# A two-block layer on one core: routing from the unnormalised residual, the first expert's places from its ranks, and two weight loads moved into the mixer

## What is computed

```python
h = h + hybrid_mixer(rmsnorm(h, norm_mix), ...)
hn = rmsnorm(h, norm_ffn)                      # x * rsqrt(mean(x*x) + eps) * g
g_logits = hn @ w_router_group                 # 256 x 4
g_idx = argmax(g_logits); g_w = softmax(g_logits)[g_idx]
e_sel = (hn @ w_router_expert)[group g_idx]    # 8 logits
top_v, top_i = top_k(e_sel, 2)
gates = g_w * softmax(top_v)
# for each token and each of its two experts e:
out += gate * ((silu(hn @ w_gate[e]) * (hn @ w_up[e])) @ w_down[e])
h = h + out
```

## Time and profile before

| what | value |
|---|---|
| median of 3 runs | 996.39 us (995.67 to 996.49) |
| the profiled execution: its time | 996.21 us |
| the profiled execution: its span | 994.5 us |
| mean granted TensorE clock | 0.918 |
| PE busy, PE weight load busy | 795.2 us (80%), 604.5 us (61%) |
| DVE, ACT, POOL busy | 476.2, 315.8, 90.2 us |
| moved by DMA | 287.00 MB, mean 289 GB/s |
| chain that ended last | DMA 36%, PE 33%, issue 21%, DVE 4% |

### The profile page before, as it was taken

One profiled execution on the slowest core, in us unless ns is written; L12 is line 12 of the kernel. 1 busy time (PEld: TensorE's weight loads), 2 busy tenths in 40 slices (PEclk: granted clock), 3 DMA queues, 4 the chain that ended last, 5 costly groups with the idle time before them and its releaser, 6 DMA issues.

```text
span 994.5 us, 15637 instructions
## 1 busy us (share of the span) xinstructions
PE 795.2 (80%) x6490; PEld 604.5 (61%) x6490; DVE 476.2 (48%) x823; ACT 315.8 (32%) x513; POOL 90.2 (9%) x111
## 2 busy tenths in 40 slices
PE   6999999998946475646636566577998999999996
PEld 6989998775624243333413334244887888888884
DVE  5856849555322031312203122125747687766775
ACT  6754355631100000000000000004485454444443
POOL 1039554100000000000000000000001010000000
PEclk9999999999988687878879798689999999999998
DMA  9984334458999999999999999999852556555101
GB/s 306 315 289 165 129 127 170 150 203 342 383 426 426 430 427 424 430 426 426 426 426 428 427 426 426 428 426 389 283 168 87 176 184 189 209 196 169 43 2 42
DMA packets 70773, 287.00 MB, mean 289 GB/s; under 512 B 11521, under 2 KB 36398, under 8 KB 58414
## 3 DMA queue, kind: packets, MB, share of 16 engines
q1 hardware_dynamic: 70386, 285.38, 72.9%
q10 hardware_dynamic: 316, 0.58, 0.2%
HBM read 284.90 MB, written 1.05 MB: 288 GB/s over the span
## 4 chain that ended last, share of the span: by engine, by line
DMA 36%; PE 33%; issue 21%; DVE 4%; POOL 3%; ACT 3%; SPq 0%; POOLq 0%; DVEq 0%; ACTq 0%
DMA down_a<-in_w_down_dram 29%; PE bank L575 12%; PE bank L624 5%; PE bank L2072 5%; DMA pair_d<-in_w_up_dram 4%; PE bank L603 3%; PE bank L2055 2%; DMA ring<-in_w_down_dram 2%; PE bank L2045 1%; DVE act_p L522 1%; DVE w_lo L560 1%; PE bank L1902 1%; ACT w_hi L550 1%; POOL seg_r L860 1%; PE bank L612 1%
## 5 line engine op out<-in xcount | busy, mean ns | idle before, releaser
L560 DVE TENSOR_TENSOR w_lo<-ring,w_hi 128x1024 fp32r<-128x1024 f32 x137 | 176.8, 1291 | 118.7 <-ACT w_hi L550 118.5
L550 ACT ACTIVATE w_hi<-ring 128x1024 fp32r<-128x1024 f32 x138 | 146.1, 1059 | 186.6 <-PE bank L575 65.0
L575 PE MATMUL bank<-act_p,w_hi 128*128 128x256 f32 x736 | 141.1, 293 | 8.0 <-issue 7.7
L1610 DVE COPY y_e<-bank 32x256 f32<-32x256 f32 x64 | 27.2, 424 | 239.0 <-PE bank L2072 238.6
L575 PEld LDWEIGHTS bank<-act_p,w_hi 128*128 128x128 f32 x736 | 118.4, 197 | 10.7 <-issue 9.9
L591 PE MATMUL bank<-act_p,w_hi 128*128 128x512 f32 x352 | 122.0, 397 | 0.0
L1118 ACT ACTIVATE y_e<-bank 32x256 f32<-32x256 f32 x64 | 23.9, 374 | 283.3 <-PE bank L2072 282.9
L575 PE MATMUL bank<-act_p,w_lo 128*128 128x256 f32 x368 | 106.1, 288 | 0.0
L2072 PE MATMUL bank<-down_a,h_t 128*32 128x256 f32 x512 | 44.8, 509 | 71.0 <-DMA down_a<-in_w_down_dram 59.7
L2055 PE MATMUL bank<-ring,x_t 128*32 128x256 f32 x1536 | 94.2, 400 | 8.8 <-issue 8.0
L624 PE MATMUL bank<-w_hi,act_q 128*128 128x512 f32 x304 | 95.3, 394 | 0.4 <-issue 0.4
(11 more groups left out here) (356 smaller groups left out, 1032.4 us busy)
## 6 DMA issues: line engine op xcount, KB each, us to landing
ring<-in_w_up_dram SPq DMA_DIRECT2D x24, 2048.0 KB, 35.5
ring<-in_w_gate_dram SPq DMA_DIRECT2D x24, 2048.0 KB, 31.0
down_a<-in_w_down_dram SPq DMA_DIRECT2D x16, 2048.0 KB, 26.1
ring<-in_w_in_dram SPq DMA_DIRECT2D x15, 2048.0 KB, 18.8
down_b<-in_w_down_dram SPq DMA_DIRECT2D x15, 2048.0 KB, 26.1
ring<-in_w_ffn_in_dram SPq DMA_DIRECT2D x22, 1024.0 KB, 6.8
pair_d<-in_w_gate_dram SPq DMA_DIRECT2D x8, 2048.0 KB, 30.1
pair_d<-in_w_up_dram SPq DMA_DIRECT2D x8, 2048.0 KB, 34.9
```

Source lines behind the costliest of these rows:

```text
L550: nc.scalar.activation(parts(w_hi, g, view), view, ACT.Copy).then_inc(split_hi, 1)
L560: engine.tensor_tensor(parts(w_lo, g, view), view, h, ALU.subtract).then_inc(split_lo, 1)
L575: mm = nc.tensor.matmul(dst, parts(wt, g, grans[g][1])[:, k, :], a[:, x_part, k, :], start=(k == 0 and i == 0), stop=(k == KC - 1 and i == 2))
L1610: ins = nc.vector.tensor_copy(y_e[CAP * e:CAP * (e + 1), 256 * j:256 * (j + 1)], bank[2][CAP * j:CAP * (j + 1), 0:256])
```

## The change

Four parts, all between the last quarter of the first mixer and the second expert:

1. **Loads.** `down_a` no longer shares its place with the routing tiles, which become views of `y_e` and `gmat`. Its first load stands behind the third of the six halves; the gate half of `pair_d` stands ahead of the sixth and waits for grain 56, the up half and `down_b` stay behind the mixer.
2. **Routing from `res`.** PE transposes the residual itself (read with a step of 8 elements) as soon as it is added. POOL multiplies `w_rt` with the gain beforehand. The norm's factor is positive and the same for all logits of a token, so the choice does not need it; it goes into the exponentials as their scale. ACT writes both blocks of `tok` beside the routing.
3. **Fewer linked steps.** The best and second of all four groups are found at once, beside the choice of the group; the ranks are divided by 32 with comparisons; gates and number of rounds are worked out later, and the engines load the number after the second group.
4. **First expert.** Expert 0's places are its ranks. A one-hot of 32 columns (`onehot[:, 1]`) is built from them, PE gathers those 32 rows first (`gather_first`), starts the product per half, and gathers the other 96 afterwards. 6 `keep_running` steps stand where there were 14.

```diff
+    down_a = sb("down_a", [P, UNIT], where=ph)
+    rt = y_e[:, 0:12 * TB * NE].rearrange("p (n b e) -> p n b e", n=12, b=TB)
+    r8 = y_e[:, 12 * TB * NE:14 * TB * NE + 32].rearrange("p (n b e) -> p n b e", n=10, b=TB)
+    r1 = y_e[:, 15 * TB * NE:15 * TB * NE + 16 * TB].rearrange("p (n b) -> p n b", n=16)
+    m_lt = gmat[:, 0:P]
...
+    TOK_BANK = ((4, 5), (7, 0))
+    LOGIT_BANK = (6, 1)
...
             load_half(i, n, i)
+            if (i, n) == (0, 1):
+                sp.wait_ge(sc_sum, KC)
+                sp.wait_ge(silu_done, XC)
+                sp.wait_ge(v_used, KC)
+                load_down(0, 0)
+            if (i, n) == (2, 1):
+                sp.wait_ge(gran_used, G_WO + 12)
+                load_half(3, 0, 3)
         sp.wait_ge(gran_used, GA)
-        load_half(3, 0, 3)
         load_half(3, 1, 3)
         load_down(1, 1)
-        sp.wait_ge(routed, 1)
-        load_down(0, 0)
...
+        nc.gpsimd.tensor_tensor(w_rt[:, :, :], w_rt[:, :, :], bcast(g_ffn[:, :].unsqueeze(2), [P, KC, NG + NE]), ALU.mult)
...
         act.wait_ge(res_mix, 1)
-        norm_act(act, 1, res, tok, (res_mix, 2), turned_rows=True)
-        for c in range(0, KC, 2):
-            act.wait_ge(tok_turned, c + 1)
-            nc.scalar.activation(tok_t[:, c, :], bank[c % 4][:, 0:T], ACT.Copy,
-                                 scale=g_ffn[:, c:c + 1]).then_inc(tok_act, 1)
-        act.wait_ge(neg_abs, 3)
-        nc.scalar.activation(r8[:, 5, :, 0:NG], r8[:, 4, :, 0:NG], ACT.Exp).then_inc(exp_ready, 1)
+        nc.scalar.activation(tok[:, 0, :], res[:, 0, :], ACT.Square, accum_out=sm[:, 0:1])
+        act.wait_ge(tok_turned, 1)
+        nc.scalar.activation(*turned_out(0, 0), ACT.Copy).then_inc(tok_act, 1)
+        act.wait_ge(tok_turned, 4)
+        nc.scalar.activation(*turned_out(1, 1), ACT.Copy).then_inc(tok_act, 1)
+        act.wait_ge(res_mix, 2)
+        nc.scalar.activation(tok[:, 1, :], res[:, 1, :], ACT.Square, accum_out=sm[:, 1:2]).then_inc(ss_act, 1)
+        act.wait_ge(rstd_ready, 2)
+        act.wait_ge(ss_act, 2)
+        for b in range(TB):
+            ins = nc.scalar.activation(by_chunk(tok[:, b, :], True), by_feature(res[:, b, :], True), ACT.Copy,
+                                       scale=sm[:, 4 + b:5 + b])
+        ins.then_inc(nrm_act, 1)
         act.wait_ge(neg_abs, 4)
-        nc.scalar.activation(r1[:, 5, :], r1[:, 4, :], ACT.Exp).then_inc(exp_ready, 1)
-        act.wait_ge(routed, 1)
-        n_more = act.value_load(rounds_i[0:1, 2:3], min_val=NE // 8 - 1, max_val=NE // 8 * (T // CAP) - 1)
+        for b in range(TB):
+            nc.scalar.activation(r8[:, 5, b, 0:NG], r8[:, 4, b, 0:NG], ACT.Exp, scale=sm[:, 4 + b:5 + b])
+            ins = nc.scalar.activation(r1[:, 5, b:b + 1], r1[:, 4, b:b + 1], ACT.Exp, scale=sm[:, 4 + b:5 + b])
+        ins.then_inc(exp_ready, 1)
...
-        dve.wait_ge(res_mix, 2)
-        norm_dve(dve, 1, res, tok, turned_rows=True)
-        for c in range(1, KC, 2):
-            dve.wait_ge(tok_turned, c + 1)
-            nc.vector.tensor_scalar(tok_t[:, c, :], bank[c % 4][:, 0:T], g_ffn[:, c:c + 1], None,
-                                    ALU.mult).then_inc(tok_dve, 1)
+        for b, h in ((0, 1), (1, 0)):
+            dve.wait_ge(tok_turned, 2 * b + h + 1)
+            nc.vector.tensor_copy(tok_t[:, 4 * h:4 * h + 4, b * P:(b + 1) * P],
+                                  bank[TOK_BANK[b][h]][:, :].rearrange("p (c t) -> p c t", c=4)).then_inc(tok_dve, 1)
...
         for b in range(TB):
-            ins = nc.vector.tensor_copy(lgt[:, b, :], bank[6 + b][:, 0:NG + NE])
+            dve.wait_ge(logits_raw, b + 1)
+            nc.vector.tensor_copy(by_group(G_LOGIT)[:, b, :], bank[LOGIT_BANK[b]][:, 0:NG])
+            ins = nc.vector.tensor_copy(rt[:, 10, b, :], bank[LOGIT_BANK[b]][:, NG:NG + NE])
+            if b == 0:
+                dve.wait_ge(ss_act, 2)
...
+        nc.vector.tensor_reduce(g_top, by_group(G_LOGIT), AX_X, ALU.max)
+        link_dve(dve, nc.vector.tensor_reduce(groups(TOP_1), experts(10), AX_X, ALU.max))
+        nc.vector.tensor_tensor(by_group(G_EQ), by_group(G_LOGIT), by_token(g_top, NG), ALU.is_equal)
+        link_dve(dve, nc.vector.tensor_tensor(experts(0), experts(10), of_group(groups(TOP_1)), ALU.is_equal))
+        nc.vector.scalar_tensor_tensor(out=by_group(G_AT), in0=by_group(G_EQ), scalar=-100.0, in1=iota_g,
+                                       op0=ALU.mult, op1=ALU.add)
+        link_dve(dve, nc.vector.scalar_tensor_tensor(out=experts(1), in0=experts(0), scalar=-100.0, in1=iota_e,
+                                                     op0=ALU.mult, op1=ALU.add))
+        nc.vector.tensor_reduce(g_at, by_group(G_AT), AX_X, ALU.min)
+        link_dve(dve, nc.vector.tensor_reduce(groups(AT_1), experts(1), AX_X, ALU.min))
+        nc.vector.tensor_tensor(by_group(G_HOT), by_group(G_AT), by_token(g_at, NG), ALU.is_equal)
+        link_dve(dve, nc.vector.tensor_tensor(experts(5), experts(1), of_group(groups(AT_1)), ALU.is_equal))
...
+        first_rank = r8[:, 9, :, 0]
+        link_dve(dve, nc.vector.tensor_copy(first_rank, bank[5][:, 0:TB * NE].rearrange("p (b e) -> p b e", b=TB)[:, :, 0]))
+        for b in range(TB):
+            ins = nc.vector.tensor_scalar(onehot[:, 1, b, 0:CAP], iota_f[:, 0:CAP], r8[:, 9, b, 0:1], rt[:, 4, b, 0:1],
+                                          ALU.is_equal, ALU.mult)
+        ins.then_inc(member, 1)
...
+        def rounds():
+            dve.wait_ge(rank_raw, 2)
+            most, over, more = r1[:, 8, 0:1], r8[:, 0, 0, 0:7], r1[:, 9, 0:1]
+            link_dve(dve, nc.vector.tensor_reduce(most, bank[7][:, 0:NE], AX_X, ALU.max))
...
+        def gate_weights():
+            dve.wait_ge(exp_ready, 4)
...
+            if before is None:
+                keep_first(0)
...
+            if before is None:
+                keep_first(1)
+                gates()
+                rounds()
+                gate_weights()
+                dve.wait_ge(routed, 1)
...
+        def keep_first(half):
+            dve.wait_ge(xt_raw, half + 1)
+            nc.vector.tensor_tensor(
+                x_t[:, 0, 4 * half:4 * half + 4, 0:CAP],
+                bank[(6, 1)[half]][:, 0:4 * CAP].rearrange("p (c j) -> p c j", c=4),
+                bcast(g_ffn[:, 4 * half:4 * half + 4].unsqueeze(2), [P, 4, CAP]), ALU.mult).then_inc(xt_kept, 1)
...
-        keep_running(5)
-        pe.wait_ge(res_mix, 2)
-        pe.wait_ge(nrm_act, 2)
-        pe.wait_ge(nrm_dve, 2)
-        for c in range(KC + 2):
-            if c < KC:
-                if c >= 4:
-                    pe.wait_ge(*((tok_act, (c - 4) // 2 + 1) if c % 2 == 0 else (tok_dve, (c - 5) // 2 + 1)))
-                for b in range(TB):
-                    mm = nc.tensor.transpose(bank[c % 4][:, b * P:(b + 1) * P], tok[:, b, c * P:(c + 1) * P],
-                                             ident[:, :])
-                mm.then_inc(tok_turned, 1)
-            if c >= 2:
-                k = c - 2
-                pe.wait_ge(tok_act if k % 2 == 0 else tok_dve, k // 2 + 1)
-                for b in range(TB):
-                    mm = nc.tensor.matmul(bank[6 + b][:, 0:NG + NE], tok_t[:, k, b * P:(b + 1) * P],
-                                          w_rt[:, k, :], start=(k == 0), stop=(k == KC - 1))
-        mm.then_inc(logits_raw, 1)
-        keep_running(5)
+        for b in range(TB):
+            pe.wait_ge(res_mix, b + 1)
+            for c in range(KC):
+                mm = nc.tensor.transpose(bank[TOK_BANK[b][c // 4]][:, (c % 4) * P:(c % 4 + 1) * P],
+                                         by_feature(res[:, b, :], True)[:, :, c], ident[:, :])
+                if c % 4 == 3:
+                    mm.then_inc(tok_turned, 1)
+        pe.wait_ge(const_ready, 3)
+        for b in range(TB):
+            for c in range(KC):
+                if c % 4 == 0:
+                    pe.wait_ge(tok_act if b == c // 4 else tok_dve, b + 1)
+                mm = nc.tensor.matmul(bank[LOGIT_BANK[b]][:, 0:NG + NE], tok_t[:, c, b * P:(b + 1) * P],
+                                      w_rt[:, c, :], start=(c == 0), stop=(c == KC - 1))
+            mm.then_inc(logits_raw, 1)
+        keep_running(4)
 
         pe.wait_ge(const_ready, 4)
         pe.wait_ge(member, 1)
         nc.tensor.matmul(bank[5][:, 0:NE], m_lt[:, :], rt[:, 4, 0, :], start=True, stop=True)
-        for o, last in ((NE, m_lt), (2 * NE, ones)):
-            nc.tensor.matmul(bank[5][:, o:o + NE], ones[:, :], rt[:, 4, 0, :], start=True, stop=False)
-            mm = nc.tensor.matmul(bank[5][:, o:o + NE], last[:, :], rt[:, 4, 1, :], start=False, stop=True)
-        mm.then_inc(rank_raw, 1)
-        keep_running(4)
-
-
-        pe.wait_ge(routed, 1)
-        n_more = pe.value_load(rounds_i[0:1, 2:3], min_val=NE // 8 - 1, max_val=NE // 8 * (T // CAP) - 1)
+        for dst, last in ((bank[5][:, NE:2 * NE], m_lt), (bank[7][:, 0:NE], ones)):
```

(30 more changed lines are left out.)

171 lines of the change are left out of this document (87 added, 84 removed).

## The result

| | before | changed |
|---|---|---|
| median | 996.39 us (994.18 to 998.07, 5 runs) | 988.11 us (985.46 to 988.88, 5 runs) |
| profiled execution, span | 994.5 us | 985.7 us |
| mean granted TensorE clock | 0.918 | 0.910 |
| PE, DVE, ACT busy | 795.2, 476.2, 315.8 us | 793.1, 473.9, 318.1 us |
| mean DMA rate | 289 GB/s | 291 GB/s |

A forecast was written before the change was run, and what follows sets the result against it. The prediction took the experts' weight stream, started by expert 0's gate-up product, to bound the kernel: product 9.3 us earlier, less a 0.2 us hole, gives 9.1 off the 996.39 median, 987.3 us, range 984.5 to 990.5.

The forecast's parts named there:

- loads have drained by: DMA queue behind the mixer: the loads ahead of the expert stream end at 233.5, some 7 us before expert 0's product.
- transposes end: PE's 16 strided transposes of res, priced at DVE's rate: 0.18 us each, 2.9 us together, done at 222.2.
- logits to the first reduction: Routing: 32 PE instructions take 3.4 us, to 225.6; after the copies DVE's first reduction starts at 226.1.
- sum of both choices: DVE's routing: the shortened chain choosing the experts takes 3.7 us, so this sum starts at 229.8 instead of 235.31.
- dummies end, gather starts: PE: two keep_running steps ahead of expert 0's gather take 1.7 us, to 233.0, ending 1.3 us after the one-hot.
- SyncE's first issue: Load queue: the expert loop's first load is issued at 240.4 instead of 249.71, following expert 0's earlier product.
- cost of the hole: DMA gap behind the loop's first issue: 10.0 us of PE work against 9.84 us of bytes, about 0.2 us lost.
- Nothing arrives: Rival: the stream's rate or a later wait gives the gain back, last load lands at 679; 996.4 us, chance 0.04.
- slow transposes: Rival: PE reads res with the step at ACT's 2.2 ns an element, 1.6 us more; 988.9 us, chance 0.12.
- a clock under 1.00 before 245: Sign against the forecast: TensorE's granted clock falling below 1.00 before 245 us would show it wrong.
- A wide hole: Rival: DVE's work between the two gathers ends 3 us late, PE waits and DMA idles; 990.3 us, chance 0.10.
- The clock rival: TensorE's clock falls to 1.2 GHz before the gather, with fewer dummies; gathers and products double, 1003.7 us, chance 0.03.

The follow-up runs named there:

- e4: The kernel before with down_a apart from the routing tiles and the two loads moved early, routing and gather as they were; ratio 0.9996 to before, median 996.21 us.
- e3: The changed kernel with both moved loads put back behind the mixer; median 988.51 us, ratio 0.9919 to the kernel before.
- e5: The changed kernel with 32 transposes of res, strided and contiguous eights alternating, in place of the four dummy matmuls behind the logits; 988.93 us in one run.
- c1: The changed kernel measured again without edits, beside a new series of the kernel before; median 987.12 us, ratio 0.9912 to before.
- e6: The changed kernel with SyncE's first loop turn written out, half a load ahead of the first down product's wait; 984.66 us, ratio 0.9888 to before.
- e6b: Repeat, in another series, of the changed kernel with half a load ahead of the first down product's wait; 985.38 us, ratio 0.9905 to before.
- e1: The changed kernel without the two keep_running steps ahead of the first gather; median 990.01 us, ratio 0.9940 to the kernel before.
- e7: The changed kernel without any keep_running step between mixer and experts; median 990.84 us, ratio 0.9947 to the kernel before.
- e8: The changed kernel with the whole first group of 128 columns gathered from pos ahead of expert 0's product; 984.53 us, ratio 0.9882 to before.

## Why the prediction was right, and where it was off

It gave 987.3 us, 984.5 to 990.5, and faster; measured are 988.11 (and 987.12 and 987.80 when repeated). By its steps, with the profile of the changed kernel:

| step | forecast | trace |
|---|---|---|
| stream sets the end, tail unchanged | 315 us | 315.15 before, 314.3 now |
| loads have drained by | 233.5 | about 235 (share 0.56 from 234, 0.09 from 235 to 236) |
| transposes end | 222.2 | 221.5 |
| logits to the first reduction | 226.1 | 225.83 |
| sum of both choices | 229.8 | 229.43 |
| ranks start | 230.2 | 230.21 |
| dummies end, gather starts | 233.0 | 233.04 |
| product starts | 236.5 | 236.63 |
| SyncE's first issue | 240.4 | 240.50 |
| next issue | 10.0 later | 9.80 later |
| cost of the hole | 0.2 | 1.0 to 1.6 |

**The frame held.** The gain is the time by which expert 0's product comes earlier, and the moved loads only make room: e4 has the loads without the gain, e3 the gain without the loads, less 1 to 2 us (the prediction priced that at 2.5). *Nothing arrives* is out.

**Two steps of the path were off and cancelled, which is luck.** The transposes were priced by DVE's 1.41 ns a column, 2.9 us; they took 1.94, what contiguous ones take, the lower bound. The rows of ACT and DVE with such a step said nothing about PE's pace. The page "SBUF — State Buffer" of the Trainium skill, section "Door 1: The DMA port swizzle", has each access to a new 16-byte line pay a penalty. The trace of e5 agrees for PE's weight loads, some 190 ns with the step and 140 without, but not for the time: the loads overlap, and the pace stays at 0.11 us. So for the sum the measurement decides, and *slow transposes* is out. In exchange the logits took 3.8 instead of 3.4 and the dummies 4.9, as the clock fell from 224.5 on, a case the sum didn't have in that place; a 2.4 GHz execution (c1) has its first issue 0.65 us sooner, counted from the mixer's end. That the forecast of 240.4 met 240.50 is thus no proof of each step. By the prediction's own signs, a clock under 1.00 before 245 would have been wrong: the profile has it at 0.50 from 225 to 228, at a small price only because it fell on dummies.

**The mis-sized term is the hole.** "A hole of about 0.2 us" compared 10.0 us of PE work with 9.84 us of bytes. The interval came as forecast, 9.80; it should by that reckoning have left no hole at all. Yet 0.3 MB are missing from the 30 us behind the first issue (0.7 us), and the whole stretch is 1.0 to 1.6 us longer, until half a load fills the gap (429.97 in e6 and in e6b). Two near-equal numbers don't make a closed queue: the next load has to be there with something to spare. The bytes behind are all lost between 11.5 and 14 us after the first issue (0.25 MB, 0.6 us) and stay so many to the end of the stream, so what is left of the 1.0 to 1.6 us isn't in the rate and was not found. How little to spare would do was not measured; 1.8 us (e6, the next issue 8.05 behind the first) was enough.

**The rivals.** *A wide hole* by DVE's lateness didn't come: `xt_kept` was waited for 0.43 us at 244.68, less than the 0.78 allowed. The clock rival was right that the clock can fall here and wrong about its condition. It was held off because PE's path has no long pause ("no gap on PE's path above exceeds about 2 us"), but in six of the ten profiles of kernels with the changed routing and no dummies taken out (in e5 transposes stand for the first four) the clock fell while PE was busy. It cost 0.65 us in the changed kernel, 4.0 in e6 with two falls (23.90 against 19.91 in e6b), and 3.4 in e1's gather and product, not the 16.4 reckoned for gathers, products and down together. No time came near the slower side.

**What bounds the gain.** Dummies ahead of the gather hold it 1.3 us, and dropping them gained nothing (e1, e7). The split gather of the fourth part is worth nothing that was seen (e8). The best two versions measured can't be told apart: the changed kernel with the hole filled, 984.66 and 985.38 in two series, which in the pieces of an execution without a fall of the clock is at 449.88 against 451.08 to 451.65, and the variant with the plain first gather, 984.53 and 986.66, with far less code.

## What to carry to other kernels

Where a stream of weights bounds a stage, look for the one event that frees its first buffer, and then at the interval from that event to the next: work that is moved out from ahead of the first often lands ahead of the second, and a queue that just covers it on paper runs dry. Loads moved into idle DMA time gain nothing until the consumer gets earlier. Price an operand's access pattern by a row of the same engine, and keep dummy matmuls until a run without them shows what the clock does.
